# A block of mixers and gated networks on one core: rounded weights released sooner, and another order in the last eight attention units

## What is computed

```python
x = x + token_mixer(rmsnorm(x, g), ...)      # four attentions, gated and mixed
x = x + conv_ffn(rmsnorm(x, g), ...)
for l in range(2):
    h = h + 0.5 * swiglu(rmsnorm(h, ffn1_norm), ...)
    z = rmsnorm(h, mix_norm) @ w_in
    y_a = mla_mixer(...)                # softmax attention, 4 heads, 4 blocks of 128 queries
    y_b = spatial_gating_mixer(z_u, z_v, ...)   # gelu, layernorm, a 128 x 128 mix, times u
    y_c = hgrn2_mixer(hq, hf, hi, hg, ...)      # recurrence, group norm, silu gate
    y_d = retention_mixer(rq, rk, rv, rg, ...)  # retention, group norm, silu gate
    h = h + concatenate([y_a, y_b, y_c, y_d]) @ w_out
    h = h + 0.5 * swiglu(rmsnorm(h, ffn2_norm), ...)
    h = h + (p @ ple_w_proj) * sigmoid(rmsnorm(h, ple_norm) @ ple_w_gate)
out = rmsnorm(h, final_norm)
```

## Time and profile before

| | us |
|---|---|
| median of 3 runs (3085.78 to 3087.28) | 3087.2 |
| the profiled execution's own time | 3087.12 |
| its span, first to last instruction | 3085.8 |
| PE busy in it | 3028.1 |
| POOL busy in it | 2221.9 |
| DVE busy, ACT busy | 1453.6, 734.7 |

### The profile page before, as it was taken

The page is one execution under the profiler, slowest core; times in us unless marked ns, Lnnn a source line. Parts: engine busy times, 40 slices in busy tenths (PEclk is TensorE's granted clock), DMA queues, the critical chain, the costliest instruction groups (busy, mean ns, idle before and its releaser), DMA issues.

```text
span 3085.8 us, 38263 instructions
## 1 busy us (share of the span) xinstructions
PE 3028.1 (98%) x14622; PEld 2462.4 (80%) x14622; DVE 1453.6 (47%) x2132; ACT 734.7 (24%) x1466; POOL 2221.9 (72%) x2524
## 2 busy tenths in 40 slices
PE   8999999999999999999999999999999999999998
PEld 7776777888888888887688888888888876888886
DVE  5367656777157421476633322533223766433214
ACT  3433222222021100344411101311003444211003
POOL 5665668999788877654487777877777443877775
PEclk9999999999999999999999999999999999999999
DMA  5222223333333333321133333333333121333332
GB/s 154 77 66 69 72 82 89 96 96 98 101 95 106 96 96 97 89 57 53 54 97 96 96 105 93 96 96 96 101 96 95 51 54 42 103 96 96 109 97 82
DMA packets 469054, 272.83 MB, mean 88 GB/s; under 512 B 20782, under 2 KB 465120, under 8 KB 468872
## 3 DMA queue, kind: packets, MB, share of 16 engines
q1 hardware_dynamic: 465704, 266.17, 29.3%
q10 hardware_dynamic: 3168, 4.22, 0.4%
HBM read 268.21 MB, written 2.12 MB: 88 GB/s over the span
## 4 chain that ended last, share of the span: by engine, by line
PE 92%; DVE 4%; ACT 2%; POOL 1%; issue 0%; DMA 0%; SPq 0%; DVEq 0%; POOLq 0%; ACTq 0%
PE bank L711 18%; PE bank L718 18%; PE bank L712 18%; PE bank L1233 6%; PE bank L1234 6%; PE bank L1239 6%; PE bank L823 1%; PE bank L824 1%; PE bank L756 1%; PE bank L757 1%; PE bank L829 1%; DVE arena L2292 1%; PE bank L1402 1%; DVE arena L2301 1%; PE bank L1090 1%; PE bank L759 1%
## 5 line engine op out<-in xcount | busy, mean ns | idle before, releaser
L668 POOL TENSOR_TENSOR wl<-raw,wh 128x256 fp32r<-128x256 f32 x2016 | 1673.0, 860 | 42.1
L663 POOL TENSOR_SCALAR wh<-raw 128x1024 fp32r<-128x1024 f32 x504 | 550.8, 1093 | 800.3 <-PE bank L718 308.8
L711 PE MATMUL bank<-xh,wh 128*128 128x512 f32 x1552 | 610.8, 394 | 3.1 <-DVE arena L2296 1.6
L712 PE MATMUL bank<-xl,wh 128*128 128x512 f32 x1552 | 604.3, 389 | 0.0
L2292 DVE TENSOR_TENSOR arena<-arena 128x512 f32<-128x512 f32 (+1 forms) x373 | 383.4, 1034 | 63.0 <-ACT arena L1998 11.7
L2292 DVE TENSOR_TENSOR arena<-bank,nrm 128x512 f32<-128x512 f32 x236 | 152.4, 685 | 512.1 <-PE bank L718 511.7
L718 PE MATMUL bank<-xh,wl 128*128 128x512 f32 x1552 | 390.8, 391 | 0.6 <-POOL wl L668 0.6
L711 PEld LDWEIGHTS bank<-xh,wh 128*128 128x128 f32 x1552 | 291.8, 188 | 66.2 <-issue 3.8
L718 PEld LDWEIGHTS bank<-xh,wl 128*128 128x128 f32 x1552 | 289.9, 188 | 65.3 <-issue 3.8
L712 PEld LDWEIGHTS bank<-xl,wh 128*128 128x128 f32 x1552 | 291.6, 188 | 60.3 <-issue 1.2
L711 PE MATMUL bank<-arena_rounded,wh 128*128 128x512 f32 x824 | 321.9, 391 | 2.2 <-DVE arena L2292 2.2
(11 more groups left out here) (366 smaller groups left out, 4157.4 us busy)
## 6 DMA issues: line engine op xcount, KB each, us to landing
raw<-in_ffn_w_gate SPq DMA_DIRECT2D x176, 256.0 KB, 3.1
raw<-in_ffn_w_up SPq DMA_DIRECT2D x176, 256.0 KB, 3.0
raw<-in_ffn_w_down SPq DMA_DIRECT2D x176, 256.0 KB, 3.0
raw<-in_w_in SPq DMA_DIRECT2D x158, 256.0 KB, 3.1
raw<-in_w_up SPq DMA_DIRECT2D x88, 256.0 KB, 3.1
raw<-in_w_gate SPq DMA_DIRECT2D x64, 256.0 KB, 3.0
raw<-in_w_out SPq DMA_DIRECT2D x48, 256.0 KB, 2.9
raw<-in_w_down SPq DMA_DIRECT2D x44, 256.0 KB, 3.0
```

The costliest lines, as they stand in the source:

```text
L663: pool.tensor_scalar(wh[:, s, :], raw[:, s, :], 1.0, 0.0, ALU.mult, ALU.add).then_inc(split, 1)
L668: ins = pool.tensor_tensor(wl[:, s, c], raw[:, s, c], wh[:, s, c].bitcast(F32), ALU.subtract)
L711: pe.matmul(psum, cols(wh, i), xhi, start=(i == 0), stop=False)
L712: pe.matmul(psum, cols(wh, i), xlo, start=False, stop=False)
```

## The change

1. **Release.** A new semaphore, `rounded_read`, is raised by the last product that reads a piece's `wh` (by two, where two pieces are used at once). POOL waits for it before it writes `wh` of the piece after next, and waits for `pieces_used` only behind that, before `wl`. Nothing is added on PE but the signal on a product that is there already; the order of PE's instructions is the same, row for row.
2. **DVE in the last units.** The layer norm of one block moves ahead of `ret_w` in unit 6, those of two in unit 7. Retention's first norm and gate move from unit 9 to unit 8, ahead of the peak of unit 10. `spatial_out(0)` moves from unit 11 to behind the peak of unit 13; operands 6 and 0 from unit 11 to behind the peak of 14; operand 2 from there to the end of unit 13, operand 3 to behind the peak of 15; the recurrence's gate from behind the peak of 15 to the start of `between(14)`.
3. **ACT.** In unit 13 the copy of the turned probabilities comes ahead of the exponentials of unit 14; the rounding of operand 3 goes from unit 12 to unit 13.

```diff
+TURNED_FIRST = 13
...
             if n >= 2:
+                pool.wait_ge(rounded_read, n - 1)
+            pool.tensor_scalar(wh[:, s, :], raw[:, s, :], 1.0, 0.0, ALU.mult, ALU.add).then_inc(split, 1)
+
+            pool.wait_ge(split, 2 * n + 1)
+            if n >= 2:
                 pool.wait_ge(book.sems["pieces_used"], n - 1)
-            pool.tensor_scalar(wh[:, s, :], raw[:, s, :], 1.0, 0.0, ALU.mult, ALU.add).then_inc(split, 1)
-
-            pool.wait_ge(split, 2 * n + 1)
...
-        def products(psum, cols, rhs, wait=True, middle=None):
+        def products(psum, cols, rhs, wait=True, middle=None, whole=True):
...
                 pe.matmul(psum, cols(wh, i), xhi, start=(i == 0), stop=False)
-                pe.matmul(psum, cols(wh, i), xlo, start=False, stop=False)
+                ins = pe.matmul(psum, cols(wh, i), xlo, start=False, stop=False)
+            if whole:
+                ins.then_inc(rounded_read, 1)
...
@@ ACT, attention
             for u in range(NH * TT):
-                if u + 1 < NH * TT:
+                copy_first = u == TURNED_FIRST
+                if u + 1 < NH * TT and not copy_first:
                     expo(u + 1)
                 n = (head_block(u)[1] + 1) * P
                 act.wait_ge(*A.at("turned", tag, u))
                 act.activation(lprobT[:, u % 2, 0:n], PT[:, 0:n], ACT.Copy).then_inc(*A.up("probT", tag, u))
+                if copy_first:
+                    expo(u + 1)
...
-                if u == 12:
-                    for i in (2, 3):
-                        act.wait_ge(*A.at("sg_out", i - 2, l))
-                        lout_first(i)
+                if u in (12, 13):
+                    i = u - 10
+                    act.wait_ge(*A.at("sg_out", i - 2, l))
+                    lout_first(i)
...
@@ DVE, between
-                if u in (11, 12):
-                    spatial_out(u - 11)
+                if u == 12:
+                    spatial_out(1)
+                if u == 13:
+                    lout_rest(2)
                 if u == 14:
+                    last()
+                    rows_out(("hg", l), hgate)
                     rstd(bank[3][:, :], ("r", 1, l))
...
-                if u == 11:
-                    for i in (6, 0):
-                        lout_rest(i)
...
-                if u == 9:
+                if u == 8:
                     rstd(bank[3][:, :], ("r", 0, l))
                     gated_group(0)
-                    last()
+                if u == 9:
                     x, y, t = sgst[:, :, 1], sgst[:, :, 3], sgst[:, :, 4]
...
+                if u in (6, 7):
+                    v.wait_ge(*V.at("zv", l))
+                    layer_norm(2 * u - 12)
+                    if u == 7:
+                        layer_norm(3)
                 if 4 <= u < 8:
...
+                if u == 6:
+                    layer_norm(1)
...
-                if u in (6, 7):
-                    v.wait_ge(*V.at("zv", l))
-                    layer_norm(2 * u - 12)
-                    layer_norm(2 * u - 11)
...
             def behind_peak(u):
+                if u == 13:
+                    spatial_out(0)
                 if u == 14:
-                    for i in (2, 3):
+                    for i in (6, 0):
                         lout_rest(i)
                 if u == 15:
-                    last()
-                    rows_out(("hg", l), hgate)
+                    lout_rest(3)
```

More of the change, by code:

```diff
@@ L438, in program @@
     SC, PT, OB = bank[4:6], bank[6], bank[7]
-    names = ["tensor_done", "vector_done", "scalar_done", "landed0", "landed1", "pieces_split", "pieces_used",
+    names = ["tensor_done", "vector_done", "scalar_done", "landed0", "landed1", "pieces_split", "pieces_used", "rounded_read",
              "loads", "first_loads", "row_loads", "x_landed0", "x_landed1", "x_landed2", "x_landed3", "const_landed",
@@ L454, in program @@
     used_at = Count(book, None, "piece_of_products")
+    rounded_read = book.sems["rounded_read"]
     load_at = Count(book, None, "piece_of_loads")
@@ L661, in _ @@
             if n >= 2:
-                pool.wait_ge(book.sems["pieces_used"], n - 1)
+                pool.wait_ge(rounded_read, n - 1)
             pool.tensor_scalar(wh[:, s, :], raw[:, s, :], 1.0, 0.0, ALU.mult, ALU.add).then_inc(split, 1)
             pool.wait_ge(split, 2 * n + 1)
+            if n >= 2:
+                pool.wait_ge(book.sems["pieces_used"], n - 1)
             for q in range(4):
@@ L757, in fm_steps @@
                     ins = pe.matmul(o, w_hi, xlo, start=False, stop=False)
+                    if end == DC and i == order[-1]:
+                        ins.then_inc(rounded_read, 1)
                     if not ahead:
@@ L772, in gemm_half, with token_major @@
             piece_used(ins, *(("gemm", *key) if b else ("gemm0", *key)))
-        def token_major(s, rhs, cols, both_parts=None, middle=None):
+        def token_major(s, rhs, cols, both_parts=None, middle=None, pieces=2):
             last = len(rhs) - 1
@@ L783, in token_major @@
                         pe.matmul(out[i], xhi[:, t], cols(wh, j), start=(j == 0), stop=False)
-                        pe.matmul(out[i], xlo[:, t], cols(wh, j), start=False, stop=False)
+                        ins = pe.matmul(out[i], xlo[:, t], cols(wh, j), start=False, stop=False)
+                if tiles[0] == 1:
+                    ins.then_inc(rounded_read, pieces)
                 if both_parts:
@@ L823, in grains_fm @@
                     pe.matmul(o, cols(wh, i), xhi, start=(i == 0), stop=False)
-                    pe.matmul(o, cols(wh, i), xlo, start=False, stop=False)
+                    ins = pe.matmul(o, cols(wh, i), xlo, start=False, stop=False)
+                    if i == last:
+                        ins.then_inc(rounded_read, 1)
                     if i in (last // 2, last):
@@ L847, in grains_tm @@
                         pe.matmul(out[i], xhi[:, t], wh[:, :, j * P:j * P + P], start=(j == 0), stop=False)
-                        pe.matmul(out[i], xlo[:, t], wh[:, :, j * P:j * P + P], start=False, stop=False)
+                        ins = pe.matmul(out[i], xlo[:, t], wh[:, :, j * P:j * P + P], start=False, stop=False)
+                    if i == TT - 1:
+                        ins.then_inc(rounded_read, 2)
                     yield
@@ L980, in first @@
                 pe.matmul(o[b], wh[:, b, c], gained[i][0], start=(i == 0), stop=False)
-                pe.matmul(o[b], wh[:, b, c], gained[i][1], start=False, stop=False)
+                ins = pe.matmul(o[b], wh[:, b, c], gained[i][1], start=False, stop=False)
+                if i == DC - 1:
+                    ins.then_inc(rounded_read, 1)
             def second(b, i):
@@ L1021, in second_slab @@
                 pe.matmul(bank[2 * s][:, :], cols(wh, i), xhi, start=(i == 0), stop=False)
-                pe.matmul(bank[2 * s][:, :], cols(wh, i), xlo, start=False, stop=False)
+                ins = pe.matmul(bank[2 * s][:, :], cols(wh, i), xlo, start=False, stop=False)
+                if i == DC - 1:
+                    ins.then_inc(rounded_read, 1)
                 if i == 4:
@@ L1131, in branch @@
                     middle()
-                ins = products(bank[2 * s + c][:, :], piece_cols(c * P, 256), rhs2)
+                ins = products(bank[2 * s + c][:, :], piece_cols(c * P, 256), rhs2, whole=(c == 1))
             piece_used(ins, "gemm", *key)
@@ L1233, in first @@
                             pe.matmul(bank[2 * s + b][:, :], w, xhi, start=(kk == 0 and i == 0), stop=False)
-                            pe.matmul(bank[2 * s + b][:, :], w, xlo, start=False, stop=False)
+                            ins = pe.matmul(bank[2 * s + b][:, :], w, xlo, start=False, stop=False)
+                        if b and g % 2:
+                            ins.then_inc(rounded_read, 1)
                     def second(b):
@@ L1310, in latent_queries @@
                 for b in range(2):
-                    ins = products(bank[2 * s + b][:, :], piece_cols(b * P, NH * MLA_D), q_in)
+                    ins = products(bank[2 * s + b][:, :], piece_cols(b * P, NH * MLA_D), q_in, whole=False)
                     if b == 0:
@@ L1330, in latent_keys @@
                 for b in range(2):
-                    ins = products(bank[2 * s + b][:, :], piece_cols(b * P, 512), kv_in)
+                    ins = products(bank[2 * s + b][:, :], piece_cols(b * P, 512), kv_in, whole=False)
                 ins.then_inc(*T.up("gemm", "uk", l))
@@ L1337, in latent_values @@
                 s = slab_start(("uv", l))
-                ins = token_major(s, kv_in, piece_cols(256, 512, 256))
+                ins = token_major(s, kv_in, piece_cols(256, 512, 256), pieces=1)
                 piece_used(ins, "gemm", "uv", l)
```

## The result

| | before | after |
|---|---|---|
| median (us) | 3086.9 | 3070.1 |
| lowest to highest | 3085.8 to 3087.3 | 3068.4 to 3071.0 |
| the profiled execution's own time | 3087.12 | 3070.95 |
| its span | 3085.8 | 3069.6 |

The ratio is 0.9944 (95% interval 0.9929 to 0.9959): 16.8 us faster. The forecast was 3076.0 with a range from 3073.6 to 3082.

A forecast was written before the change was run, and what follows sets the result against it. PE was taken to bound the kernel, busy 3028.1 of 3085.8 us. Gains of 2.3 + 2.2 + 6.8 = 11.3 us, less 0.2, made 11.1 off 3087.12: forecast 3076.0, range 3073.6 to 3082.

The forecast's parts named there:

- Part 1, the first block: First block: earlier release of POOL's rounding gains 1.35 us behind the values and 1.0 at remainders, taken as 2.3.
- Part 2, the mixers: Mixers of both layers: earlier release of POOL's rounding gains 1.1 us a layer, 2.2 in all.
- unit 1 would give its 1.12 back: Mixers, unit 1: PE arrives 1.1 us sooner but waits that long for ACT's copy at the values; 0.1 counted.
- the single-piece products of each mixer: Mixers: short waits before a single-piece product, a few tenths, would end with the release; 0.25 us a layer.
- the two waits for remainders: First block: two PE waits for POOL's remainders, 1.0 us together, would go because POOL starts two microseconds sooner.
- The price of a signal: Some 490 PE products carry one more signal, at price 0; the rival, a slower program, had chance 0.04.
- Part 3: Units 7 to 9: reordered DVE work gains 1.3 us a layer at unit 9's values, plus 1.7 from the clock.
- The walk: Step-by-step timing of DVE, ACT and PE through units 7 to 9: PE resumes at 1484.45, not 1485.77; gain 1.3.
- the second number: Behind unit 9's wait: PE's clock stays high, gaining 1.7 us a layer; the low-clock rival had chance 0.15.
- Part 4: Units 10 to 15: only 0.4 us a layer is added to the 3.0 gained earlier; waits move to unit 15.
- the walk's two roads: End of mixers: DVE's chain brings operand 7 at 1514.05, PE's own road through unit 15 ends at 1513.3.
- The 0.2 for other collisions: Whole program: 0.2 us taken off the summed gain for POOL and DVE meeting at other places.

The follow-up runs named there:

- experiment 1: Kernel before with only the release and its signals, DVE and ACT in their old order: 3077.0 us, ratio 0.9967.
- experiment 4: Kernel before with all signals, but early release only for pieces used two at a time, DVE and ACT as before: 3082.1 us, ratio 0.9985.
- experiment 3: Kernel before with the new signals on PE's products but POOL waiting as before: 3087.2 us, ratio 1.000.
- experiment 10: The change with unit 13's copy of turned probabilities back behind the exponentials of unit 14: 3071.2 us, ratio 0.9947.
- experiment 11: The change with the recurrence's gate back behind the peak of unit 15, ahead of its shares: 3070.8 us, ratio 0.9947.
- experiment 2: The change with only the new DVE and ACT order, POOL's waits and PE's signals as before: 3082.6 us, ratio 0.9985.
- experiment 9: On top of experiment 8, operands 6 and 0 rounded in unit 9 and their remainders made in unit 10: 3065.4 us, ratio 0.9927.
- experiment 5: The change with the layer norms back behind the retention weights (weighting of the scores): 3080.9 us, ratio 0.9981.
- experiment 6: The change with retention's first norm and gate back in unit 9, layer norms still early: 3075.8 us, ratio 0.9962.
- experiment 7: The change with the copy of turned probabilities ahead of the next exponentials in units 1 and 9 too: 3066.3 us, ratio 0.993.
- experiment 8: On top of experiment 7, the recurrence's gate, its silu and operand 7 moved later: 3064.3 us, ratio 0.9926.

## Why the prediction was wrong in size and right in kind

- **Part 1, the first block: 2.3 forecast, 5.6 measured. The step that failed** is the reading of the list of waits, where I let the releaser's name say which waits the release could end. By the names POOL had one of 1.4 and two remainders of 1.0 in all. It had two more, of 1.14 and 1.03, put down to DVE, which ended 0.12 us later. Experiments 1 and 4 show that the first is POOL's; for the second it is shown by the fourth, which takes it away with an unchanged DVE. These two are 2.4 us.
- **Part 2, the mixers: 2.2 forecast, 5.4 measured.** The same step failed at 1351.83, a wait of 0.46 named DVE that ends 0.15 us behind POOL and 0.03 behind DVE: 0.70 a layer. That unit 1 would give its 1.12 back was right: +1.31, then -1.03.
- **The same step, its size.** A wait that ended mostly gave more than its length: 1.59 for 1.35, 1.26 for 1.03, 1.31 for 1.12, 0.70 for 0.46, 0.50 for 0.26. The shown idle begins where the product before it ends, 0.39 us after its start, while in a row the next product begins at 0.23; so 0.16 of a wait lies under that product, and the first product behind a wait takes 0.07 more. These 0.23 are about the excess. Where PE couldn't close up fully there is little of it: 1.16 for 1.14, where the product still starts 0.34 us behind the transposes, and 0.79 for 0.75. Of the 6.4 us that I missed in parts 1 and 2, 3.8 stood at waits that weren't named POOL's, and 2.6 came at the places I had counted, 1.3 of them at the single-piece products of each mixer (0.90 where I had taken 0.25) and 0.55 at the two waits for remainders.
- **The price of a signal: 0 forecast, 0 measured** (experiment 3).
- **Part 3: 1.3 and 1.7 a layer forecast; +1.37 and +1.53 measured** in layer 0, +1.36 and +1.52 in layer 1. The walk held to 0.12 us at four instructions. But the second number owes something to luck. After a wait of about the same length (2.35 to 2.54 us), windows at unit 9 of layer 0 and of layer 1 read a clock of 1.00 in experiment 4, and of 0.57 and 1.00 in experiment 1. A kernel with that wait doesn't always pay for the clock.
- **Part 4: 0.4 a layer forecast, 0.26 and 0.67 measured.** The three waits came where they were said: 1.06 and 0.95 where about 1 was walked, and 1.13 and 0.77 (layer 0 and 1) at operand 7 where the walk's two roads left 0.75. That the copy of unit 13 is worth little was shown by experiment 10, that the gate's place is too by experiment 11.
- **The 0.2 for other collisions** is 1.6 at three places in the networks (-0.47, -0.64, -0.46), where PE waits longer for DVE. They are there in experiment 1 too and not in experiments 2 and 4, so they come with the release of single pieces; what collides there stays open.
- **The range** was built from what could fall short of the forecast and reached 2.4 us below it. The unknown that mattered, whose a wait is, had an upper side as well: the waits named DVE at products that read `wh` were in the list, 1.6 and 1.1 and 0.9 us among them, and the range should have reached to them.
- **Luck in the sum.** The steps of the parts make 10.9 + 6.7 = 17.6, and the profiled time fell by 16.2. They are that near only because the rest nearly cancels in this execution: +1.2 in its first 50 us, -2.05 at 277 to 302, and the small steps of the networks.

## What to carry over

Where a wait ends on an instruction that needs two engines, look at when both ended before you believe the name: within 0.15 us of each other either may be the releaser, and the one that isn't named becomes the gain, or the loss, that the list doesn't show. Then compare with waits of the same trace whose cause is plain: here PE started 0.15 us behind POOL's rounding and about 0.05 behind DVE, and the distance told which it was. Count a wait that is removed as its length and up to 0.2 us more. In a chain written by hand, an edit that is good for the next wait can be bad for the one behind it, so walk on until two engines meet again, and ask of each step what is queued behind it as well as who waits for it.

Of the versions tried, the copy ahead of the exponentials in units 1, 9 and 13, with or without the later gate, is faster than the kernel before and the change: 3066.3 and 3064.3 us.

## What the hardware showed that was not expected

The granted clock fell at places that differ from one execution to the next. Windows at 269.5 us of the change and at 478 us of experiment 2, columns as above:

```profile
269.50:273.50 4.00, 3.97 (x23) 3.27 (x24) 3.63 (x14) 2.16 (x6) 0.00 (x0) 0.57 0.21 59
```
```profile
478.00:482.00 4.00, 4.00 (x12) 3.09 (x12) 3.43 (x6) 1.23 (x2) 0.02 (x1) 0.57 0.46 135
```

The first stands behind a wait of 0.52 us, the second behind waits of 1.36 and 0.16. Neither wait decides it. The kernel before has waits of 1.36 and 0.18 at the second place and no such stretch. The wait of 0.52 or 0.53 at the first is in nine of the executions: the clock fell behind it in the change and in experiments 1, 9 and 10, and stayed at 1.00 in experiments 5 to 8 and 11. Where it falls, it reads 0.50 of full speed, 1.2 GHz in place of 2.4, and PE comes out 1.5 to 1.6 us later each time (1.57 of the -2.05 at 277 to 302 us in the table above; the rest are waits). And behind one and the same wait of 2.4 us at unit 9 it fell in some executions and not in others:

```profile
1478.00:1482.00 4.00, 4.00 (x13) 2.77 (x12) 3.83 (x6) 0.00 (x0) 0.00 (x0) 0.57 0.44 131
2572.00:2576.00 4.00, 4.00 (x19) 3.02 (x20) 3.72 (x7) 0.00 (x0) 0.05 (x1) 1.00 0.45 135
```

(both of experiment 1, layer 0 and layer 1, behind waits of 2.36 and 2.35 us). With the first 50 us, in which the profiled executions differ by up to 1.65 us, these stretches are most of what two profiles differ by where the program is the same. That is why a profiled execution's steps add up to its own time only, and a difference of 1 us between two kernels needs more than one profile. What decides whether the clock falls stays open; no run here was made for it.
